# Remainders of the second MLP's weight tiles: an accumulating DMA onto a sign-turned tile in place of GpSimd's subtraction

## The chip, the cores and the metric

The kernel runs on one core of one Trainium2 chip. The metric is the device time of one execution in microseconds; the shown time is the median of three runs. One further execution was taken by the hardware profiler, and every row below is from it.

## The reference, cut to what matters

One inference step of a two-layer decoder over 512 prompt tokens and 8 x 4 sample tokens (544 columns in all), D = 1024. Layer 0 mixes by an mLSTM, layer 1 by a gated short convolution; each is followed by a squared-ReLU MLP. The change touches only the MLP of layer 1 (and the way its weights are prepared):

```
hn = modulate(x, norm_g[i, 1], mod[:, 3], mod[:, 4])
f = jnp.square(jax.nn.relu(hn @ mlp_w_up[i])) @ mlp_w_down[i]     # 1024 -> 4096 -> 1024
x = x + mod[:, 5][:, None, :] * f
```

All of it is float32.

## The kernel before

Activations lie transposed, features on the partitions and the 544 tokens along the row. Every large product is made of weight tiles of 1024 x 128 values: 192 of them, numbered `t` through the whole kernel, 8 to a unit. A float32 product is built from three products in the reduced format fp32r: the weight is split into a rounded part `wh` and a remainder `wl = raw - wh`, the activation likewise into `Xh, Xl` (or `Hh, Hl`), and TensorE adds `wh*Xh + wh*Xl + wl*Xh` into PSUM. One tile is 8 k-steps x 3 products x 2 halves of the tokens, 48 matmuls.

A weight tile passes four hands:

1. SP fetches it, 512 KB, from HBM into `raw[t % 2]` (`fetch`, L359). `raw` has two buffers (`RAWS`), so SP waits first until the remainder of tile t-2 is done (L358).
2. ScalarE rounds it: `wh[t % 4] <- raw[t % 2]` (`hi`, L465), once the tile is there and once TensorE has finished tile t-4, which held the slot (`SLOTS` = 4).
3. GpSimd subtracts: `wl[t % 4] <- raw - wh` (`lo`, L851), once step 2 is done, and signals `s_lo`.
4. TensorE waits for `s_hi` and `s_lo` of the tile (`split_wait`) and runs its 48 matmuls.

The engines' queues are in order. ScalarE's queue interleaves `hi(t+3)` (`LEAD` = 3) and the evacuation of tile t: in an up unit (relu into one of two `stage` buffers, L472 or L485) that is an activation; in a down unit ScalarE evacuates nothing, and VectorE adds the product to the residual (L1009, L1014, L1016). In an up unit VectorE squares the staged result and splits it (`drain_square`: L991, L992, L998). PSUM holds two tiles (`slot(g)`), so tile g starts only when g-2 has been evacuated.

The MLP of layer 1 is the last part of the kernel: tiles 128 to 191 (`T_MLP1` to `T_END`), eight units, up and down by turns. A unit's first two tiles run in step (`tile_pair`, matmuls at L1589), since their activations come one k at a time from VectorE; the other six run one after another (`tile`, L1563). The first up unit is special (`first_unit`): its first three tiles run on the raw x, scaled afterwards (`scale_first`), while VectorE and ScalarE still make the normalized operand (`norm_apply`, L1153, L1167; `norm_hi`, L621). GpSimd has besides one small power per norm (`norm_power`, L861).

The order of ScalarE's work in all units but the first, and the split's wait, in the kernel's words:

```
for m in range(KT):
    hi(t0 + m + LEAD, j, per_t)
    ...
    if evac is not None:
        evac(t0 + m, g0 + m, j, per_t, per_g)
```

Of the kernel before, what the change touches and what calls it, by code (L numbers as in the profile page):

```python
# [15 lines left out]
ALU = mybir.AluOpType  # L16
ACT = mybir.ActivationFunctionType
# [19 lines left out]
SLOTS, RAWS, ADAS, LEAD = 4, 2, 2, 3  # L37
# [13 lines left out]
T_CG, T_XT, T_BG, T_COUT, T_MLP1, T_MLP1_LAST, T_END = 96, 104, 112, 120, 128, 176, 192  # L51
G_QK, G_V, G_O, G_WOUT, G_MLP0, G_MLP0L, G_MLP0_LAST = 0, 8, 16, 24, 32, 48, 80
G_CG, G_XT, G_BG, G_COUT, G_MLP1, G_MLP1_LAST = 96, 104, 112, 120, 128, 176

ADA_AFTER = {1: 0, 3: 1, 5: 2, 6: 3}
ADA_AFTER_O = {2: 0, 4: 1, 5: 2, 6: 3}
ADA_AFTER_W = {1: 0, 3: 1, 4: 2, 5: 3}
# [44 lines left out]
def build_program(nc, ins, outs):  # L102
    ctx = ExitStack()
    with ctx:
# [3 lines left out]
        def sb(name, shape, dt=F32, at=None):  # L108
            n = 4
            for s in shape[1:]:  # L110
                n *= s
            n = (n + 31) // 32 * 32
            if at is None:
                at = mark["at"]
                mark["at"] += n
            return nc.alloc_sbuf_tensor_at(name, shape, dt, offset=at)
# [6 lines left out]
        def sem(name):  # L123
            return ctx.enter_context(nc.semaphore(name))
# [36 lines left out]
        raw = sb("raw", [P, RAWS, KT, P])  # L161
# [3 lines left out]
        wl = sb("wl", [P, SLOTS, KT, P], F32R, at=at_w + SLOTS * D * 4)  # L165
# [110 lines left out]
        s_au = sem("ada_tile_used")  # L276
        s_hi = sem("hi_ready")
        s_lo = sem("lo_ready")
        s_used = sem("tile_used")
        s_ev = sem("evacuated")  # L280
        s_dr = sem("drained")
# [53 lines left out]
        def at(n, j, per):  # L335

            return n if j is None else j * per + n

        def split_wait(eng, t, j, per):

            eng.wait_ge(s_hi, at(t + 1, j, per))
            eng.wait_ge(s_lo, at(t + 1, j, per))

        def ada_fetch(queue, a):

# [8 lines left out]
        def _(sp):  # L354
            def fetch(t, w, c, j=None, per=0):

                if t >= RAWS:
                    sp.wait_ge(s_lo, at(t - RAWS + 1, j, per))  # L358
                nc.sync.dma_start(raw[:, t % RAWS], w.rearrange("(k p) n -> p k n", p=P)[:, :, bass.ds(c, P)])\  # L359
                    .then_inc(s_raw[t % RAWS], 16)  # L360

            def unit(t0, w, c0, j=None, per=0, order=range(KT)):
                for m in order:
                    fetch(t0 + m, w, c0 + P * m, j, per)
# [23 lines left out]
            for a in range(H // 2):  # L388
                fetch(T_V + 3 + a, w_in, D + P * (3 + a))
                nc.sync.dma_start(C0[:, :, a, 0:DV], state_rows(ins["state_mlstm_C"][0], a)).then_inc(s_sin, 16)  # L390
# [20 lines left out]
            for a in range(H // 2):  # L411
                fetch(T_MLP0 + a, up[0], a * P)
                if a < H // 2 - 1:
                    sp.wait_ge(s_upd, SB * (a + 1))
                else:
                    sp.wait_ge(s_cud, 1)
                nc.sync.dma_start(state_rows(outs[6][0], a), C0[:, :, a, 0:DV]).then_inc(s_out, 16)
# [35 lines left out]
        def _(act):  # L453
            chain = Count(act, s_a)

            def hi(t, j=None, per=0):

                if t >= T_END:
                    return
                act.wait_ge(s_raw[t % RAWS], at(16 * (t // RAWS + 1), j, per // RAWS * 16))  # L460
                if t >= SLOTS:
                    act.wait_ge(s_used, at(t - SLOTS + 1, j, per))
                else:
                    act.wait_ge(s_au, 8)
                nc.scalar.activation(wh[:, t % SLOTS], raw[:, t % RAWS], ACT.Copy).then_inc(s_hi, 1)  # L465

            def to_stage(func, free=None, **kw):
# [109 lines left out]

            def mixed(t0, g0, n, evac, j=None, per_t=0, per_g=0, per_n=0, after={}, ada_after=ADA_AFTER, raw_of=None):

                for m in range(KT):  # L580
                    t = t0 + m
                    if t != T_QK and m != 1:
                        hi(t + LEAD, j, per_t)
                    if m == 0:
                        hi(t + 1 + LEAD, j, per_t)
                    if evac is not None:
                        evac(t, g0 + m, j, per_t, per_g)
                    if m in after:
                        after[m]()
                    if raw_of is not None and m:  # L590
                        raw_hi(raw_of, m - 1)
                    if n >= BATCH:
                        if m in BATCH_AT:
                            batch_next(n, BATCH_AT.index(m))
                    elif m in ada_after:
                        ada_next(4 * n + ada_after[m])
# [35 lines left out]
            for dst, src in pin:  # L632
# [4 lines left out]
                                 scale=-1.0).then_inc(s_silu, 1)  # L637
# [198 lines left out]
            for j in range(2):  # L836
                scale = rms[:, 1, j:j + 1]
# [5 lines left out]
        def _(pool):  # L843
            chain = Count(pool, s_p)

            def lo(t, j=None, per=0):

                if t >= T_END:
                    return
                pool.wait_ge(s_hi, at(t + 1, j, per))  # L850
                nc.gpsimd.tensor_tensor(wl[:, t % SLOTS], raw[:, t % RAWS], wh[:, t % SLOTS].bitcast(F32),  # L851
                                        ALU.subtract).then_inc(s_lo, 1)

            def lows(t0, t1, j=None, per=0):
                for t in range(t0, t1):
                    lo(t, j, per)
# [101 lines left out]
            pool.wait_ge(s_diag, 3)  # L958

            lo(T_CG + LEAD)  # L960
            pool.wait_ge(s_used, T_CG + 2)
            nc.gpsimd.memset(u[:, :, 0:2], 0.0).then_inc(s_cre, 1)
# [582 lines left out]
        def _(pe):  # L1545
# [5 lines left out]
            def tile(t, g, xh, xl, j, per_t, per_g, between=None, before_last=None):  # L1551

                s = t % SLOTS
                split_wait(pe, t, j, per_t)
                if g >= 2:
                    pe.wait_ge(s_ev, at(g - 1, j, per_g))
                for k in range(KT):
                    first, final = k == 0, k == KT - 1
                    if final and before_last is not None:
                        before_last()  # L1560
                    for w, x, st, en in ((wh, xh, first, False), (wh, xl, False, False), (wl, xh, False, final)):
                        for hf in range(2):
                            last = mm(G[:, 2 * (g % 2) + hf, 0:HALF], w[:, s, k, :], x[:, k, hf * HALF:(hf + 1) * HALF],  # L1563
                                      start=st, stop=en)
                    if final:
                        last.then_inc(s_used, 1)
                    if between is not None:
                        between(k)
# [8 lines left out]
            def pair_steps(t, g, xh, xl, width, order, free, ready, between=None):  # L1577

                for k, o in order:
                    if k == 0:  # L1580
                        split_wait(pe, t + o, None, 0)
                        free(o)
                    if o == 0:
                        ready(k)
                    s, q = (t + o) % SLOTS, 2 * ((g + o) % 2)
                    first, final = k == 0, k == KT - 1
                    for w, x, st, en in ((wh, xh, first, False), (wh, xl, False, False), (wl, xh, False, final)):
                        for hf in range(2):
                            last = mm(G[:, q + hf, 0:width], w[:, s, k, :], x[:, k, hf * width:(hf + 1) * width],  # L1589
                                      start=st, stop=en)  # L1590
                    if final:
                        last.then_inc(s_used, 1)
                    if between is not None:
                        between(k, o)
# [77 lines left out]

            def mixed(t0, g0, n, xh, xl, ready, j=None, per_t=0, per_g=0, per_n=0, post=None, between=None, ada_after=ADA_AFTER):
                for m in range(KT):
                    t = t0 + m
                    if m == 0 and ready is not None:
                        tile_pair(t, g0, xh, xl, j, per_t, per_g, ready)
                    if m > 1 or ready is None:
                        tile(t, g0 + m, xh, xl, j, per_t, per_g, None if between is None else between(m))
                        if post is not None:  # L1680
                            post(m)
                    if n < BATCH and m in ada_after:
                        ada_pair(4 * n + ada_after[m])
                if n >= BATCH:
                    ada_batch(n)
# [358 lines left out]
```

## Time and profile before

| | |
|---|---|
| time, median of 3 runs | 1353.19 us (1352.53 to 1353.42) |
| span of the profiled execution | 1352.8 us |
| TensorE (PE) busy | 1313.0 us, 97% |
| VectorE (DVE) busy | 720.8 us, 53% |
| ScalarE (ACT) busy | 361.7 us, 27% |
| GpSimd (POOL) busy | 528.5 us, 39% |
| DMA, mean | 125 GB/s |
| weight tiles in the second MLP | 64 of 192 |

PE is TensorE's matmul part and PEld its weight load. The busy share is an average over stages; a matmul's end is modelled in the profile. The span and the median differ by 0.4 us, so a sum made on the span can be read as one on the median.

### The profile page before, as it was taken

How to read it: one execution, taken by the hardware profiler on the slowest of the kernel's cores; microseconds unless marked ns; L12 is line 12 of the kernel's file. 1: busy time of each engine (PE TensorE's matmuls, PEld its weight loads, DVE VectorE, ACT ScalarE, POOL GpSimd, SP SyncE). 2: the span in 40 equal slices, each digit the busy share in tenths (PEclk: the TensorE clock that was granted, in tenths of full speed). 3: DMA queues.
4: the chain of work that ended last, by engine and by line, in shares of the span. 5: the costliest groups of instructions: out<-in, count | busy, mean ns of one | idle time of the engine just before them, and what ended most of it. 6: DMA issues, size and time to landing. Idle time of an engine off the chain costs nothing.

```text
span 1352.8 us, 26364 instructions
## 1 busy us (share of the span) xinstructions
PE 1313.0 (97%) x11593; PEld 1287.1 (95%) x11593; DVE 720.8 (53%) x1120; ACT 361.7 (27%) x560; POOL 528.5 (39%) x248
## 2 busy tenths in 40 slices
PE   5899999999999999999999999999999999999996
PEld 4799999999999999999999999999999999999996
DVE  2723445577951631541559619769861641741774
ACT  3532452121411211211222422122421221221211
POOL 2434433443343434334334344443443443433540
PEclk9899999999999999999999999999999999999998
DMA  9666214753465655555533133322223233232321
GB/s 333 193 196 155 76 53 118 237 166 117 150 194 156 185 158 157 166 166 154 170 112 94 56 101 96 88 87 78 77 80 94 80 92 94 79 93 79 94 63 66
DMA packets 239804, 169.34 MB, mean 125 GB/s; under 512 B 5691, under 2 KB 211775, under 8 KB 239562
## 3 DMA queue, kind: packets, MB, share of 16 engines
q1 hardware_dynamic: 215946, 121.33, 30.5%
q10 hardware_dynamic: 23584, 46.27, 10.5%
q8 instruction: 91, 1.49, 0.5%
q14 instruction: 23, 0.19, 0.0%
q0 software_dynamic: 160, 0.07, 0.0%
HBM read 160.70 MB, written 6.94 MB: 124 GB/s over the span
## 4 chain that ended last, share of the span: by engine, by line
PE 83%; DVE 10%; issue 3%; ACT 1%; DMA 1%; POOL 0%; SPq 0%; POOLq 0%; DVEq 0%; ACTq 0%
PE G L1563 55%; PE G L1589 20%; PE B L1659 3%; DVE hb L1153 1%; DVE acc L1030 1%; PE B L1549 1%; DVE small_s L1503 1%; DVE yc L1502 1%; DMA xin<-in_x_sample 1%; DVE Xl L1167 1%; PE B L1828 1%; DVE Hl L998 1%; DVE Hh L991 1%; PE B L1843 1%; PE B L1855 1%
## 5 line engine op out<-in xcount | busy, mean ns | idle before, releaser
L851 POOL TENSOR_TENSOR wl<-raw,wh 128x1024 fp32r<-128x1024 f32 x192 | 487.8, 2544 | 666.0 <-ACT wh L465 663.0
L465 ACT ACTIVATE wh<-raw 128x1024 fp32r<-128x1024 f32 x192 | 202.8, 1056 | 486.6 <-PE G L1563 231.9
L1563 PE MATMUL G<-Xh,wh 128*128 128x272 f32 x960 | 204.7, 295 | 1.2 <-POOL wl L851 1.2
L1563 PE MATMUL G<-Xl,wh 128*128 128x272 f32 x960 | 198.8, 288 | 0.0
L1563 PE MATMUL G<-Xh,wl 128*128 128x272 f32 x960 | 197.7, 287 | 0.0
L1563 PE MATMUL G<-Hh,wh 128*128 128x272 f32 x864 | 179.2, 289 | 0.0
L1563 PE MATMUL G<-Hl,wh 128*128 128x272 f32 x864 | 178.8, 288 | 0.0
L1563 PE MATMUL G<-Hh,wl 128*128 128x272 f32 x864 | 176.9, 286 | 0.0
L1563 PEld LDWEIGHTS G<-Xh,wh 128*128 128x128 f32 x960 | 149.8, 189 | 7.0 <-issue 4.8
L1009 DVE TENSOR_TENSOR small_s<-G,modT 128x32 f32<-128x32 f32 x80 | 15.2, 190 | 262.3 <-PE G L1563 190.3
L1563 PEld LDWEIGHTS G<-Xl,wh 128*128 128x128 f32 x960 | 151.4, 189 | 0.0
L1563 PEld LDWEIGHTS G<-Xh,wl 128*128 128x128 f32 x960 | 150.8, 189 | 0.0
L998 DVE TENSOR_TENSOR Hl<-sqb,Hh 128x544 fp32r<-128x544 f32 x72 | 143.9, 1999 | 2.5
L1563 PEld LDWEIGHTS G<-Hl,wh 128*128 128x128 f32 x864 | 136.0, 189 | 0.0
L1563 PEld LDWEIGHTS G<-Hh,wl 128*128 128x128 f32 x864 | 135.4, 188 | 0.0
L1563 PEld LDWEIGHTS G<-Hh,wh 128*128 128x128 f32 x864 | 134.7, 188 | 0.0
L991 DVE TENSOR_TENSOR Hh<-stage 128x544 fp32r<-128x544 f32 x58 | 57.2, 986 | 128.5 <-ACT stage L472 124.7
L472 ACT ACTIVATE stage<-G 128x544 f32<-128x544 f32 x64 | 40.0, 624 | 257.1 <-PE G L1563 189.6
L1563 PE MATMUL G<-Yh,wh 128*128 128x272 f32 x432 | 90.6, 291 | 0.0
L1563 PE MATMUL G<-Yl,wh 128*128 128x272 f32 x432 | 89.3, 288 | 0.0
L1563 PE MATMUL G<-Yh,wl 128*128 128x272 f32 x432 | 88.7, 286 | 0.0
L1563 PEld LDWEIGHTS G<-Yh,wh 128*128 128x128 f32 x432 | 67.3, 188 | 1.8 <-issue 1.8
(329 smaller groups left out, 2019.1 us busy)
## 6 DMA issues: line engine op xcount, KB each, us to landing
raw<-in_mlp_w_up SPq DMA_DIRECT2D x64, 512.0 KB, 4.1
raw<-in_mlp_w_down SPq DMA_DIRECT2D x64, 512.0 KB, 3.6
batch<-in_ada_w ACTq DMA_DIRECT2D x56, 512.0 KB, 5.1
raw<-in_mlstm_w_in SPq DMA_DIRECT2D x24, 512.0 KB, 4.2
raw<-in_conv_w_in SPq DMA_DIRECT2D x24, 512.0 KB, 3.7
aring<-in_ada_w ACTq DMA_DIRECT2D x22, 512.0 KB, 4.9
early<-in_ada_w SPq DMA_DIRECT2D x16, 512.0 KB, 12.3
raw<-in_mlstm_w_out SPq DMA_DIRECT2D x8, 512.0 KB, 4.9
```

The lines of the kernel that those rows point to most:

```text
L465: nc.scalar.activation(wh[:, t % SLOTS], raw[:, t % RAWS], ACT.Copy).then_inc(s_hi, 1)
L472: nc.scalar.activation(halves(stage[g % 2][:, :]), slot(g), func, **kw).then_inc(s_ev, 1)
L851: nc.gpsimd.tensor_tensor(wl[:, t % SLOTS], raw[:, t % RAWS], wh[:, t % SLOTS].bitcast(F32), ALU.subtract).then_inc(s_lo, 1)
L991: V.tensor_tensor(halves(hi_out[:, m, :]), ps, o, ALU.mult)
L998: V.tensor_tensor(lo_out[:, m, :], sqb[:, :], hi_out[:, m, :].bitcast(F32), ALU.subtract)\
L1009: mid(V.tensor_tensor(small_s[:, :].rearrange("p (h b t) -> p h b t", h=2, t=ST), ps[:, :, PH:HALF].rearrange("p h (b t) -> p h b t", t=ST ...
L1030: ins_ = V.tensor_tensor(acc[:, :], acc[:, :], sqb[:, :], ALU.add)
L1153: V.scalar_tensor_tensor(prompt(hb[k % 2][:, :]), prompt(xT[:, k, :]), gain[:, k, 0:1], prompt(xr[:, :]), ALU.mult, ALU.mult).then_inc(s_h ...
L1167: V.scalar_tensor_tensor(prompt(xl[:, k, :]), prompt(hb[k % 2][:, :]), modT[:, sh, k, 0:1], prompt(xh[:, k, :].bitcast(F32)), ALU.add, ALU ...
L1563: last = mm(G[:, 2 * (g % 2) + hf, 0:HALF], w[:, s, k, :], x[:, k, hf * HALF:(hf + 1) * HALF], start=st, stop=en)
L1589: last = mm(G[:, q + hf, 0:width], w[:, s, k, :], x[:, k, hf * width:(hf + 1) * width], start=st, stop=en)
L1659: last = mm(ada_out[GW * g:GW * (g + 1), P * quad:P * (quad + 1)], cpad[:, kk, :], columns, start=(kk == 0), stop=(kk == KT - 1), tile_pos ...
```

## The change

For tiles 128 to 191 the remainder is made in another way. ScalarE first writes the rounded tile with its sign turned into `wl` (a second activation over the same tile, ahead of the one that writes `wh`). Then GpSimd, instead of computing, issues an accumulating DMA that adds `raw` onto `wl`. Each of the four `wl` slots has a semaphore of its own; TensorE (`split_wait`) and SP (`fetch`) wait for this one in place of `s_lo`. The other 128 tiles stay as they were.

```
+T_ADDED = T_MLP1
...
+        s_lod = [sem(f"lo_added{i}") for i in range(SLOTS)]
...
             eng.wait_ge(s_hi, at(t + 1, j, per))
-            eng.wait_ge(s_lo, at(t + 1, j, per))
+            lo_wait(eng, t, j, per)
+
+        def lo_wait(eng, t, j=None, per=0):
+
+            if t >= T_ADDED:
+                eng.wait_ge(s_lod[t % SLOTS], 16 * ((t - T_ADDED) // SLOTS + 1))
+            else:
+                eng.wait_ge(s_lo, at(t + 1, j, per))
...
                 if t >= RAWS:
-                    sp.wait_ge(s_lo, at(t - RAWS + 1, j, per))
+                    lo_wait(sp, t - RAWS, j, per)
...
+                if t >= T_ADDED:
+                    nc.scalar.activation(wl[:, t % SLOTS], raw[:, t % RAWS], ACT.Copy, scale=-1.0)
                 nc.scalar.activation(wh[:, t % SLOTS], raw[:, t % RAWS], ACT.Copy).then_inc(s_hi, 1)
...
                 pool.wait_ge(s_hi, at(t + 1, j, per))
+                if t >= T_ADDED:
+                    nc.gpsimd.dma_start(wl[:, t % SLOTS], raw[:, t % RAWS], accum_op=ALU.add).then_inc(s_lod[t % SLOTS], 16)
+                    return
                 nc.gpsimd.tensor_tensor(wl[:, t % SLOTS], raw[:, t % RAWS], wh[:, t % SLOTS].bitcast(F32),
                                         ALU.subtract).then_inc(s_lo, 1)
```

## Rows read from the trace of the kernel before

**Rows 1.** Busy time by engine (us) in stretches of the second MLP.

```profile
core 0: us, PE busy (x) PEld busy (x) DVE busy (x) ACT busy (x) POOL busy (x), PEclk, DMA share, GB/s
995.00:1000.00 5.00, 3.18 (x17) 3.21 (x18) 4.72 (x6) 1.57 (x2) 2.30 (x1) 0.78 0.00 0
1000.00:1005.00 5.00, 5.00 (x37) 5.00 (x37) 2.36 (x3) 0.00 (x0) 0.42 (x1) 0.88 0.35 105
1005.00:1010.00 5.00, 5.00 (x42) 5.00 (x42) 1.14 (x4) 1.06 (x1) 1.16 (x1) 1.00 0.02 3
1046.40:1094.30 47.90, 47.49 (x380) 47.30 (x379) 29.62 (x23) 11.63 (x15) 21.24 (x8) 1.00 0.28 81
1094.30:1142.30 48.00, 47.95 (x383) 47.76 (x383) 11.75 (x24) 8.99 (x9) 19.32 (x8) 1.00 0.31 89
```

**Rows 2.** Timeline of ScalarE in an up unit: start, us, instruction, idle before.

```profile
1058.58 0.62 ACT L472 ACTIVATE stage<-G 128x544 f32<-128x544 f32 x1 [0.68 <-PE G L1589]
...
1088.58 0.62 ACT L472 ACTIVATE stage<-G 128x544 f32<-128x544 f32 x1 [4.43 <-PE G L1563]
1089.10 1.05 ACT L465 ACTIVATE wh<-raw 128x1024 fp32r<-128x1024 f32 x1
```

**Rows 3.** Timeline of GpSimd in the same unit.

```profile
1090.23 2.62 POOL L851 TENSOR_TENSOR wl<-raw,wh 128x1024 fp32r<-128x1024 f32 x1 [3.38 <-ACT wh L465]
```

**Rows 4.** Waits of SP's queue, 985 to 1345 us: total, times, longest.

```profile
SPq L359 <- POOL wl L851: 302.5, 53, 10.7
```

**Rows 5.** Fetches of L359, 1000 to 1290 us: issue to landing.

```profile
DMA to landing us min/median/max: 3.4/4.0/5.5
```

**Rows 6.** Other DMAs of the kernel: KB each, median us from issue to landing.

```profile
raw<-in_mlp_w_down SPq DMA_DIRECT2D x64, 512.0 KB, 3.6
...
xspill<-xT ACTq DMA_DIRECT2D x1, 2176.0 KB, 8.3
...
bgate<-in_mlstm_b_gates POOLq DMA_DIRECT2D x2, 0.0 KB, 5.9
crows<-in_state_conv ACTq DMA_DIRECT2D x1, 64.0 KB, 2.5
```

**Rows 7.** Timeline of GpSimd at the kernel's start: its own DMA issues.

```profile
3.40 1.16 POOL L879 DMA_DIRECT2D graw<-in_mlstm_w_in  x1 [0.30 <-POOL graw L876]
...
5.44 0.57 POOL L882 DMA_DIRECT2D bgate<-in_mlstm_b_gates  x1
```

**Rows 8.** The page: DMA engines' busy tenths in 40 slices.

```profile
DMA  9666214753465655555533133322223233232321
```

**Rows 9.** Waits of TensorE, 930 to 1353 us.

```profile
PE G L1589 <- ACT stage L485: 2.5, 1, 2.5
PE G L1589 <- ACT wh L465: 1.2, 3, 0.4
```

**Rows 10.** Timeline of VectorE in the first up unit.

```profile
972.81 2.93 DVE L992 TENSOR_TENSOR sqb<-stage 128x544 f32<-128x544 f32 x1
975.78 2.80 DVE L998 TENSOR_TENSOR Hl<-sqb,Hh 128x544 fp32r<-128x544 f32 x1
978.69 0.72 DVE L991 TENSOR_TENSOR Hh<-stage 128x544 fp32r<-128x544 f32 x1
...
995.23 0.72 DVE L998 TENSOR_TENSOR Hl<-sqb,Hh 128x544 fp32r<-128x544 f32 x1
```

**Rows 11.** Timeline of ScalarE in the first up unit.

```profile
971.38 1.05 ACT L465 ACTIVATE wh<-raw 128x1024 fp32r<-128x1024 f32 x1
...
978.92 1.06 ACT L465 ACTIVATE wh<-raw 128x1024 fp32r<-128x1024 f32 x1 [2.67 <-DMA raw<-in_mlp_w_down]
983.13 0.63 ACT L485 ACTIVATE stage<-G 128x544 f32<-128x544 f32 x1 [3.15 <-DVE Hl L998]
...
996.05 0.62 ACT L485 ACTIVATE stage<-G 128x544 f32<-128x544 f32 x1 [6.83 <-DVE Hl L998]
```

**Rows 12.** Timeline of TensorE at the first down unit's start.

```profile
996.82 0.49 PE L1589 MATMUL G<-Hh,wh 128*128 128x272 f32 x2 [2.45 <-ACT stage L485]
```

## The prediction

> **What bounds the kernel now.** I read the page first, then the busy time by stretches, then the waits of TensorE, of SP's queue and of the three other engines, and last the timelines of one unit in the middle of the second MLP and of its first up unit. TensorE is the bound: a unit of eight tiles takes 47.9 to 48.0 us and TensorE is busy for 47.5 to 47.95 of them, at full granted clock [rows 1]. So a tile costs 48.0 / 8 = 6.0 us, and all else has to keep up with one tile per 6.0 us. Over the whole stretch TensorE waits little: 2.5 us once at the end of the first up unit and three times 0.4 us where an up unit follows a down unit [rows 9]. Nothing that GpSimd does is awaited by TensorE directly, so taking 64 subtractions off GpSimd frees nothing on the path by itself.
>
> The work around the change is a ring. In the steady part ScalarE evacuates a tile at 1088.58, rounds the next one at 1089.10 (1.05 us) [rows 2], GpSimd subtracts from 1090.23 for 2.62 us, to 1092.85 [rows 3], and that frees the raw buffer for SP: its queue stands 302.5 us in 53 waits for just this [rows 4]. The fetch then lands after a median of 4.0 us [rows 5] (3.6 for the down weights of the whole kernel [rows 6]); I take 3.9. Rounding, a hop of 0.08, 2.62 and 3.9 make 7.7 us. There are two raw buffers, so a buffer may take two tiles' time, 12.0 us, for one round. It has 4.3 us to spare.
>
> **The change part by part.** *Removed:* GpSimd's 2.6 us per tile from the ring. *Added:* a second activation over the tile. It has the shape of the present one, so 1.05 us, ahead of the round-off, 64 times. ScalarE is busy for 11.6 us of 47.9 in an up unit [rows 1]; 8.4 more fit. The ring gets 1.05 us of it. *Added:* the adding DMA, from GpSimd's wait to its landing; call it X. The round is then 2 x 1.05 + 0.1 + X + 3.9 = 6.1 + X, and it fits into 12.0 us as long as X is under 5.9. Beyond that each microsecond of X costs half a microsecond per tile, 32 per kernel. All hangs on X, and the trace before has no adding DMA and none from SBUF to SBUF.
>
> Bounds for X. *Fixed part:* the shortest landings are 2.5 us for 64 KB issued from ScalarE's queue [rows 6]; GpSimd's issue of a DMA takes 0.57 us for one with few pieces and 1.16 us for one with many [rows 7]. A whole tile has 128 rows, few, so 2.5 + 0.6 = 3.1. The 5.9 us of GpSimd's own tiny DMAs [rows 6] were measured while the engines were 90% busy [rows 8]; I keep 5.9 as the upper end of the fixed part. *Moving:* a fetch of 512 KB takes the 16 engines 0.29 of 6.0 us = 1.75 us (share of the two units in rows 1). The large store, 2176 KB in 8.3 us, gives (2176 - 64) / (8.3 - 2.5) = 364 KB/us, or 1.4 us for 512 KB [rows 6]. An add reads the source and the old contents and writes once. If the reads overlap it takes 1.4 us, as two passes 3.5 us, as three 5.25 us. So X lies between 2.5 + 1.4 = 3.9 and 5.9 + 5.25 = 11.2 us. I take 3.1 + 3.5 = 6.6, two passes at the fetch's own rate, because that is the one rate measured in this stage and each byte that is added has to be read twice.
>
> The Trainium skill's page "DMA: Bandwidth & Descriptors" (section Anatomy of one DMA) fits 2.0 us plus bytes at 436 GB/s, 3.2 us for a tile, and "Collectives: The Full Stack" (section on large sizes) holds that an add in the DMA engines runs at half a copy's rate for its two source reads, which makes some 4.4 us by these pages (an estimate). No row here shows an add. By it the sum would be no loss; that outcome is a rival below.
>
> *Moved together:* the add of one buffer and the fetch into the other now share the 16 engines. With X = 6.6 the add of one tile and the fetch half a round later coincide for some of their 3.5 and 1.75 us of engine time. Fully overlapped, each is held up by what it shares, up to 1.8 us a round; kept apart, nothing. I take 0.5 us. The round becomes 6.1 + 6.6 + 0.5 = 13.2 us, 1.2 over, and there are some 30 of them in series on a buffer (32, less the first, fetched ahead, and the last, which nothing follows): 30 x 1.2 = 36 us.
>
> Slack in hand pays back a part. The second tile of a pair is needed 0.75 us after the pair's start, and its slot was freed 12 us before that start; its remainder is ready 0.5 + 2.1 + 0.1 + 6.6 + 0.5 = 9.8 us after that, 3 us early. So 3 us of lateness go by once before TensorE stands. 36 - 3 = 33 us.
>
> *The other waits that the change adds.* Behind ScalarE's longer wait for raw tiles stands the evacuation of a tile, and behind that VectorE's drain and TensorE's PSUM slot; an evacuation may be late by about 5.4 us (6.0 less 0.62) before the tile after next stands, so in the steady part the missing remainder ends first, not this. Near a pair the first two tiles end 2.25 us apart (the evacuation at 1058.58 had but 0.68 us of idle before it [rows 2]), so the two adds are issued close together and partly share the engines; that is within the 0.5 above. GpSimd's queue holds nothing else in the stage but two tiny powers; it only waits and issues.
>
> *What VectorE gains.* VectorE's operations on 128x544 take 0.72 us with GpSimd idle and 2.8 to 2.93 us while it subtracts [rows 10]. In the first up unit five such long ones stand in the chain of drains that delays the evacuation at 996.05 [rows 11], and TensorE stands 2.45 us for it [rows 12]. After that the granted clock is 0.78 and 0.88 for 10 us (a part of that time at the lower of its two levels), and 17 and 37 matmuls run where 26 (in the 3.2 us left of the stretch) and 41 to 42 would [rows 1]: 9 and 4.5 lost, at 0.125 us each 1.7 us. Together 4.1 us. With no subtraction the drains end some 10 us earlier and this wait goes, provided the weights are there. In that unit the ring is already late before: the round-off at 978.92 waited 2.67 us for its fetch [rows 11]. Following it: round-off at 971.38, now done at 973.5, add landed at 973.6 + X, fetch 3.9, round-off done at 979.6 + X, add landed at 979.7 + 2X, next fetch, and the round-off ahead of the evacuation of the last tile ends at 985.7 + 2X. That evacuation, 0.6 us, must be done by 996.8 - 2.45 = 994.4, so the 4.1 us are only won if X is at most 4.0; at X = 5 about half, at 5.9 nothing. At X = 6.6 what TensorE waits for are remainders, and I count no gain.
>
> The sum on the profiled span: 1352.8 + 33 = 1386; on the median the same to half a microsecond.
>
> **Rivals.**
> *A, the forecast:* the ring is over its 12.0 us by 0.5 to 3 us. 30 x 0.5 - 3 = 12 and 30 x 3 - 3 = 87, so 1365 to 1440, likeliest 1386. Chance 0.42.
> *B, hidden:* X with sharing is between 4.3 and 6.0 us. The lateness is taken by the slack, and a gain of 0 to 2.5 us in the first up unit stands against a few tenths of wait at pairs. 1350.5 to 1355. For it speaks the 3.1 us fixed part with 1.4 of moving, 4.5 us. Chance 0.26.
> *C, faster:* one mechanism, at the end of the first up unit: VectorE is no longer held up by GpSimd, the wait of 2.45 us and the slower clock after it go. It decides where X is 4.0 us or less: 1353.2 - 4.1 = 1349. Against it, that X must be at its lower bound. Chance 0.13. The skill's rule above (4.4 us) falls between B and C.
> *D, far over:* the fixed part for GpSimd's DMAs is really near the 5.9 us of [rows 6]: X = 5.9 + 3.5 = 9.4, with sharing a round of 16.0 us: 30 x 4.0 - 3 = 117, so about 1470, and 1520 at the upper bound. Against it, those DMAs stood in full queues. Chance 0.19.
> That the add is not made as a DMA in the background, but holds GpSimd, changes nothing: GpSimd has no other work here.
>
> **How the numbers follow.** The forecast is A's, 1386. The range takes in all of B and A and the near part of D and leaves out most of C and D's far part: 1350 to 1460, with A's own 1365 to 1440. Under 0.2%, 2.7 us, a measurement can't tell a change. Faster by more than that: 0.12, most of C. Within: 0.27, B and the rest of C. Slower: 0.61, A and D.
>
> **What would show it.** In the profile after: 64 more activations of 1.05 us at the line of the sign-turned copy; GpSimd nearly idle over the last third; VectorE's L998 at 0.72 us throughout; SP's queue waiting for the adds; the landing time of the adds, which is X (right near 6.6); ScalarE's round-off waiting for raw DMAs in nearly every tile instead of for TensorE; TensorE waiting for the adds' landing at most tiles, and a unit of 51 to 56 us. The prediction is wrong if X is under 5.9 us (units stay at 48 us), or if the adds and fetches slow each other much more than 0.5 us, or if standing for a part of each tile costs TensorE its clock, as it did after 996.

## The result and the profile after

The changed kernel takes 1370.67 us in the median of seven runs, against 1353.42 us for the kernel before, also of seven: 17 us or 1.3% slower. The ratio, which leaves out the longest run of the changed kernel (1386.9 us) as one of a slower state, is 1.010, with a 95% interval of 1.0063 to 1.0138, or 14 us. The two kernels differ in their spread too: the one before lies within 1352.5 to 1355.0 us, the changed one between 1359 and 1387 us. The direction was forecast, the size (33 us) was not.

The profiled execution took 1378.96 us with a span of 1377.2, so it is one of the longer ones: 24.4 us over the span of before. First the page: busy time by engine, TensorE's granted clock and the DMA engines' share in 40 slices, and GpSimd's own DMA queue.

```profile
PE 1319.8 (96%) x11593; PEld 1294.0 (94%) x11593; DVE 639.9 (46%) x1120; ACT 421.5 (31%) x624; POOL 420.7 (31%) x248
...
PEclk9999999999999999999999999999999999999998
DMA  9665213762663653653622332335667777778772
...
q0 software_dynamic: 9376, 33.63, 13.7%
...
raw<-in_mlp_w_up SPq DMA_DIRECT2D x64, 512.0 KB, 4.4
raw<-in_mlp_w_down SPq DMA_DIRECT2D x64, 512.0 KB, 4.0
wl<-raw POOLq DMA_DIRECT2D x64, 512.0 KB, 5.3
```

VectorE is busy for 81 us less with the same 1120 instructions: the last of its three operations per drain (L998, now L1012) takes 0.72 us each time, where it took 2.4 us in the mean from 998 to 1310 us of the kernel before. ScalarE has 60 us more. The DMA engines go from two or three tenths [rows 8] to seven in the last third. The adding DMA, the unknown of the prediction, lands 5.3 us after its issue in the median, and the fetches beside it 4.4 and 4.0 us. The add's engine time is 13.7% of 1377.2 us over 64, that is 2.95 us of all 16 engines.

Next the waits of 930 to 1377 us by engine and releaser: total, times, longest; one row of SP's queue, two of ScalarE's, then TensorE's.

```profile
SPq L368 <- DMA wl<-raw: 382.1, 61, 10.5
...
ACT wl L475 <- DMA raw<-in_mlp_w_down: 112.7, 20, 8.9
...
ACT wl L475 <- DMA raw<-in_mlp_w_up: 78.8, 20, 8.9
...
PE G L1603 <- DMA wl<-raw: 14.1, 4, 5.5
PE G L1603 <- ACT stage L483: 5.2, 2, 3.0
PE G L1603 <- ACT stage L496: 2.2, 1, 2.2
```

ScalarE, which waited for TensorE before each round-off [rows 2], now waits for fetches 40 times, and the fetches wait for adds. TensorE's waits are few and long: four for adds, 14.1 us in all, and three for evacuations, 7.4 us, all at L1603, the pairs at a unit's start. That the lateness of six tiles comes due there, since both tiles of a pair are wanted together, is how I read it; no run tests it. Counted from the first matmul of a pair to that of the next, the units from 993 to 1309 us take 54.2, 55.6, 50.8, 54.3, 52.6 and 48.7 us. Before, they took 52.2 and then 48.7 or 48.3.

The chain that ended last in the stretch from 1060 to 1145 us, in order of time, shows the ring itself. Columns: start, us, what.

```profile
1072.20 7.21 DMA wl<-raw
1079.40 0.01 issue
1079.42 4.39 DMA raw<-in_mlp_w_up
...
1086.13 6.54 DMA wl<-raw
...
1099.34 0.02 ACT wl L475
1099.37 0.07 issue
1099.44 0.02 ACTq L471
1099.45 0.85 issue
1100.31 1.05 ACT wh L476
1101.36 0.28 issue
1101.64 4.53 DMA wl<-raw
1106.17 0.02 issue
1106.19 6.34 DMA raw<-in_mlp_w_down
1112.53 0.02 issue
1112.56 1.06 ACT wl L475
```

From 1069.90 to 1138.22 no matmul is in the chain, only one raw buffer's negate, round-off, add and fetch, five rounds of 12.5 to 15.5 us where 12.0 are allowed. Such a chain picks the later buffer; the other one's rounds in the same stretch take 12.0 to 13.0 us, read from GpSimd's issues. The one shown in full takes 13.2 us, 1099.34 to 1112.56. Its add takes 4.5 us, the shortest seen, and its fetch 6.3, against 3.5 at its shortest; two rounds earlier it is the add that takes 7.2 us and the fetch 4.4. The timeline of GpSimd, with the adds of both buffers, tells why.

```profile
1072.20 0.84 POOL L863 DMA_DIRECT2D wl<-raw  x1 [3.75 <-ACT wh L476]
1079.70 0.86 POOL L863 DMA_DIRECT2D wl<-raw  x1 [6.66 <-ACT wh L476]
...
1101.64 0.84 POOL L863 DMA_DIRECT2D wl<-raw  x1 [8.32 <-ACT wh L476]
1105.13 0.85 POOL L863 DMA_DIRECT2D wl<-raw  x1 [2.64 <-ACT wh L476]
1114.85 0.84 POOL L863 DMA_DIRECT2D wl<-raw  x1 [8.87 <-ACT wh L476]
```

In the up unit the two buffers lie about half a round apart, 7.5 us, and the add of 1072.20 meets the other buffer's fetch, which SP issues at 1072.33. In the down unit they have drawn together, 3.5 us, and the second add, of 1105.13, falls first into the other add and then into the first buffer's fetch of 1106.19. They meet either way.

Last the busy time by stretches, of the changed kernel around one wait, and over six units; the row by itself is the same 300 us of a kernel that does not wait (first12_raw3, below). The columns are those of [rows 1].

```profile
1045.00:1055.00 10.00, 4.49 (x31) 4.30 (x31) 1.04 (x3) 3.90 (x4) 1.70 (x2) 0.80 0.67 142
1055.00:1060.00 5.00, 5.00 (x32) 5.00 (x31) 0.00 (x0) 1.32 (x2) 0.00 (x0) 0.72 0.92 223
...
1000.00:1300.00 300.00, 284.98 (x2214) 284.05 (x2214) 68.78 (x135) 103.67 (x115) 38.35 (x46) 0.97 0.74 162
```

```profile
1000.00:1300.00 300.00, 298.61 (x2378) 297.49 (x2378) 132.75 (x152) 65.32 (x74) 127.12 (x50) 1.00 0.30 89
```

In those 300 us TensorE runs 164 matmuls fewer than where it does not wait, 20.5 us at 0.125 us each. It is idle for only 13.6 us more. The other 7 us are the clock: after the wait of 5.5 us, which ends at 1053.61, the granted clock of the next 5 us is 0.72, so a part of them ran at the lower of the two levels (1.2 GHz instead of 2.4), and 32 matmuls ran where 42 do. Where TensorE does not stand, in the row of first12_raw3, the granted clock is 1.00.

### The profile page after: what moved, and what is told of

The parts are those of the page before. It is cut to its first block, busy times and chain, and to the rows that moved or that the text cites. A ratio compares the mean times of both kernels' runs of the same rounds, so it can differ in the third digit from the quotient of the medians.

```text
span 1377.2 us, 26428 instructions
## 1 busy us (share of the span) xinstructions
PE 1319.8 (96%) x11593; PEld 1294.0 (94%) x11593; DVE 639.9 (46%) x1120; ACT 421.5 (31%) x624; POOL 420.7 (31%) x248
## 3 DMA queue, kind: packets, MB, share of 16 engines
q0 software_dynamic: 9376, 33.63, 13.7%
## 4 chain that ended last, share of the span: by engine, by line
PE 63%; DMA 21%; DVE 7%; issue 4%; ACT 4%; SPq 0%; POOL 0%; POOLq 0%; DVEq 0%; ACTq 0%
PE G L1577 38%; PE G L1603 16%; DMA wl<-raw 9%; DMA raw<-in_mlp_w_down 6%; DMA raw<-in_mlp_w_up 4%; PE B L1673 3%; ACT wh L476 2%; PE B L1563 1%; DVE small_s L1517 1%; ACT wl L475 1%; DVE yc L1516 1%; DMA xin<-in_x_sample 1%; DVE hb L1167 1%; PE B L1842 1%; DVE acc L1044 1%
## 5 line engine op out<-in xcount | busy, mean ns | idle before, releaser
L865 POOL TENSOR_TENSOR wl<-raw,wh 128x1024 fp32r<-128x1024 f32 x128 | 325.2, 2544 | 440.7 <-ACT wh L476 438.8
L863 POOL DMA_DIRECT2D wl<-raw x64 | 54.7, 854 | 357.6 <-ACT wh L476 345.4
L1005 DVE TENSOR_TENSOR Hh<-stage 128x544 fp32r<-128x544 f32 x58 | 51.2, 883 | 203.5 <-ACT stage L483 188.0
L475 ACT ACTIVATE wl<-raw 128x1024 fp32r<-128x1024 f32 x64 | 67.7, 1057 | 225.8 <-DMA raw<-in_mlp_w_down 112.7
L1012 DVE TENSOR_TENSOR Hl<-sqb,Hh 128x544 fp32r<-128x544 f32 x72 | 94.1, 1307 | 2.5
```

Of the source, the lines that this page charges most:

```text
L475: nc.scalar.activation(wl[:, t % SLOTS], raw[:, t % RAWS], ACT.Copy, scale=-1.0)
L863: nc.gpsimd.dma_start(wl[:, t % SLOTS], raw[:, t % RAWS], accum_op=ALU.add).then_inc(s_lod[t % SLOTS], 16)
L1005: V.tensor_tensor(halves(hi_out[:, m, :]), ps, o, ALU.mult)
L1012: V.tensor_tensor(lo_out[:, m, :], sqb[:, :], hi_out[:, m, :].bitcast(F32), ALU.subtract)\
```

## The experiments

My theory at this point: the round of a raw buffer is longer than two tiles' time, by latency. The rivals: the DMA engines are short of throughput; the second activation on ScalarE is what costs; the expensive part is a DMA issued from GpSimd as such, not its adding. All times are medians, with the ratio to the kernel before on the same chip and its 95% interval.

**a_raw3: a third raw buffer for tiles 128 on.** It lies where `aring` was, dead in this part of the kernel; tile 130 finds it free, and tiles 131 on wait for the remainder of tile t-3.

```
+RAWS1 = 3
...
+        raw1 = sb("raw1", [P, RAWS1, KT, P], at=at_raw)
+
+        def raw_of_tile(t):
+            return raw1[:, (t - T_MLP1) % RAWS1] if t >= T_MLP1 else raw[:, t % RAWS]
```

> The changed kernel with three raw buffers in the second MLP (the third lies in the space of a buffer that is dead by then). Ring theory: the changed kernel lost because a raw buffer's round (negate and round off 2.0 us, add 4.5 to 7.2 us, fetch 3.5 to 6.6 us, seen as 12.5 to 15.5 us) does not fit into two tiles, 12.0 us; three buffers allow 18 us, so TensorE does not wait for weights any more and the time falls to 1349 to 1353 us, at best with the 4.1 us of the first up unit won. Engine theory (the 16 DMA engines cannot carry the adds beside the fetches): a third buffer only lets more of both queue up; the time stays at 1360 to 1380 us. ScalarE theory (the second activation delays evacuations): no change either, 1360 to 1380 us.

1347.81 us, 0.9958 (0.9946 to 0.9971): not only the loss is gone, it is 5.6 us faster than before. Its waits of TensorE from 930 to 1345 us are these two rows, and the second is at the very end:

```profile
PE G L1614 <- DVE xT L1039: 1.2, 3, 0.4
PE G L2036 <- DVE acc L1055: 0.6, 1, 0.6
```

From 1000 to 1300 us the adds (first line) and the fetches (second line) land no earlier than in the changed kernel, where their medians were 5.4 and 4.6 us, and the DMA engines carry more per microsecond (172 GB/s against 162):

```profile
DMA to landing us min/median/max: 4.5/5.7/8.2
...
DMA to landing us min/median/max: 3.5/4.7/8.1
```

So neither throughput nor the second activation is what failed: the same adds, somewhat slower ones even, are harmless where a round may take 18 us.

**b_raw3: the third raw buffer in the kernel before.** The same edit without the adds.

```
-                    sp.wait_ge(s_lo, at(t - RAWS + 1, j, per))
...
+                    sp.wait_ge(s_lo, at(t - back + 1, j, per))
```

> Control: the kernel before with the same third raw buffer. Its ring has 4.3 us to spare, so all theories expect no change, 1351 to 1354 us. If it gained, the third buffer would be worth something of its own and a_raw3 would have to be read against it.

1353.84 us, 1.0004 (0.9995 to 1.0014). The buffer has no worth of its own, and the wait of 2.4 us at the end of the first up unit stays. TensorE's granted clock stays at 1.00 after it, where it fell to 0.78 after the 2.45 us of the kernel before [rows 1]: the clock's price does not follow each such wait.

**neg_only: the second activation alone, in the kernel before.**

```
+                if t >= T_MLP1:
+                    nc.scalar.activation(wl[:, t % SLOTS], raw[:, t % RAWS], ACT.Copy, scale=-1.0)
                 nc.scalar.activation(wh[:, t % SLOTS], raw[:, t % RAWS], ACT.Copy).then_inc(s_hi, 1)
```

> The kernel before with only the added activation: the sign-turned tile is written and then overwritten by GpSimd's subtraction. Ring theory: the round is 7.7 + 1.0 = 8.7 us, under 12.0, so no change in the steady part, 1352 to 1356 us with a microsecond or two in the first up unit, where the ring was late before. ScalarE theory: most of the loss of the change, 1360 us and more.

1354.91 us, 1.0008 (0.9999 to 1.0017): 1.5 us, if anything. The ScalarE theory falls.

**plain_copy: the add as a plain copy.** The remainder is replaced by the whole tile.

```
-                    nc.gpsimd.dma_start(wl[:, t % SLOTS], raw[:, t % RAWS], accum_op=ALU.add)...
+                    nc.gpsimd.dma_start(wl[:, t % SLOTS], raw[:, t % RAWS])...
```

> The changed kernel with a plain DMA copy of raw onto the tile in place of the adding one (the remainder is then the whole tile, so this computes something else). It keeps issue, size and both waits and takes away only the second read and the addition. If accumulating is the expensive part (ring and engine theory alike): the landing falls from 5.3 us to some 3.5 to 4 us, the engines' share from 0.7 to about 0.55, and the time to 1349 to 1356 us. If a DMA issued by GpSimd is slow for its issue and its fixed part, the landing stays above 4.5 us and the time above 1358 us.

1349.9 us, 0.9972 (0.9962 to 0.9982). The page's rows on GpSimd's queue and its landing:

```profile
q0 software_dynamic: 9376, 33.63, 7.6%
...
wl<-raw POOLq DMA_DIRECT2D x64, 512.0 KB, 3.4
```

Adding costs 1.9 us of landing in the median (5.3 against 3.4), 1.6 us at the shortest (4.5 against 2.9), and nearly doubles the engine time: 7.6% of 1347.5 us over 64 is 1.60 us, against 2.95. The Trainium skill's page "Collectives: The Full Stack" (section "The bandwidth ceiling: the fold count and why AG ≠ RS ≠ AR") gives an add two source reads and half a copy's rate, a factor of two; the ratio here is 1.84. GpSimd's issue as such was not the trouble. At the end of the first up unit a wait of 1.2 us for the evacuation is left.

**half_add: an add over half the tile.** The remainder of four k-slices is left at the negative rounded tile.

```
+                    nc.gpsimd.dma_start(wl[:, t % SLOTS, 0:KT // 2], raw[:, t % RAWS, 0:KT // 2], accum_op=ALU.add)...
```

> The changed kernel with an adding DMA over four of the eight k-slices, 256 KB in place of 512 KB (the remainder of the other four stays the negative rounded tile, so this computes something else). It splits the landing into a fixed and a moving part. By the prediction's terms (3.1 fixed, 3.5 moving) it would land in 3.1 + 1.75 = 4.9 us; by the 4.5 us that an add took alone in the changed kernel and 2.4 us of it fixed, in 3.4 to 3.8 us. Ring theory: the round falls under 12 us in either case, and the time to 1348 to 1354 us.

1349.32 us, 0.9963 (0.9948 to 0.9978). The adds of 1000 to 1300 us:

```profile
DMA to landing us min/median/max: 3.2/3.7/5.8
```

The shortest landing is 3.2 us for 256 KB and 4.5 for 512 KB. That makes 1.3 us per half, so by these two shortest landings 2.6 us of moving and 1.9 us fixed for an undisturbed add. As with the plain copy, a wait of 1.2 us for the evacuation at the end of the first up unit is left.

**early_add: GpSimd issues the add before the second round-off.** Only the wait moves; SP waits for both.

```
+                    nc.scalar.activation(wl[...], raw[...], ACT.Copy, scale=-1.0).then_inc(s_neg, 1)
...
+                    pool.wait_ge(s_neg, t - T_ADDED + 1)
...
+                    if t - RAWS >= T_ADDED:
+                        sp.wait_ge(s_hi, t - RAWS + 1)
```

> The changed kernel, but GpSimd issues the add as soon as the sign-turned tile is there, while ScalarE still rounds off the second time (the add does not read that tile). SP waits for both before it fetches over the raw tile. Ring theory: the round of a raw buffer gets 1.0 us shorter, which is more than half of what it is over 12.0 us in the median, so most of the loss goes: 1350 to 1362 us, against 1360 to 1380 for the changed kernel. Engine theory (throughput, not latency): no change, 1360 to 1380 us, since as many bytes are moved.

1351.82 us, 0.9984 (0.9976 to 0.9993). One microsecond less of latency, with not a byte less to move, takes away 19 of 1371 us (16 by the ratios) and the spread with it (1348.5 to 1353.7). That is the low end of what I had expected: the ring lies near its limit. From 1000 to 1300 us TensorE loses nothing:

```profile
1000.00:1300.00 300.00, 298.61 (x2378) 297.49 (x2378) 78.97 (x154) 113.20 (x124) 42.14 (x50) 1.00 0.80 173
```

The evacuation at the end of the first up unit is still late, so the gain of that unit is not won:

```profile
PE G L1607 <- ACT stage L499: 2.9, 1, 2.9
```

**one_buffer: adds for even tiles only.** Odd tiles, in the other raw buffer, are subtracted.

```
+        def added(t):
+            return t >= T_ADDED and t % 2 == 0
```

> The changed kernel with the adding DMA only for even tiles (one of the two raw buffers); odd tiles are subtracted by GpSimd as before. Ring theory with contention as the missing part: an add never meets another add and meets a fetch more rarely, so it lands in 4.5 to 5.3 us and its ring (2.0 + 0.3 + 5 + 4 = 11.3 us) fits, the other ring needs 7.7 us: no wait for weights, 1351 to 1356 us. If the add were over 6 us by itself, the even ring would stay over 12 us and TensorE would still wait, half as much or more: 1360 us and up.

1353.75 us, 0.9999 (0.999 to 1.0008). The page's row for the adds:

```profile
wl<-raw POOLq DMA_DIRECT2D x32, 512.0 KB, 4.6
```

With no other add to meet, the landing is 4.6 us in the median (4.5 from 1000 to 1300 us), so the add alone is a 4.5 us operation and its ring fits. What is gone here is the other buffer's adds; its fetches are still there. So what lengthened an add in the changed kernel was the other buffer's traffic, most likely its adds. How much the other buffer's fetches lengthen an add no run separates.

**first12_raw3: three raw buffers, adds for tiles 128 to 139 only.**

```
+        def added(t):
+            return T_ADDED <= t < T_ADDED + 12
```

> Three raw buffers, and the adding DMA only for tiles 128 to 139, that is for the first up unit; from tile 140 on GpSimd subtracts. If the gain of a_raw3 (5.6 us) comes from VectorE running free of GpSimd in the first up unit and in the norm before it, as I hold, all of it is here too: 1347 to 1349 us. If the later units gave a part, the time lies between that and 1353 us.

Tiles 128 to 135 are the first up unit's own; the next four are prepared while it runs or just after it.

1348.26 us, 0.9961 (0.9946 to 0.9977): all of the gain of a_raw3 is in the first up unit and the norm before it; the other 52 adds give nothing. The units of a_raw3's trace say the same: the first two take 51.2 and 48.3 us against 52.7 and 52.2 before, the rest as long as before.

**first12: the same with two raw buffers.**

> The same with the two raw buffers of the kernels before and after. By the prediction's step, the evacuation at the end of the first up unit is in time only if the add lands in 4.0 us; measured were 4.5 to 5.7. So part of the gain: 1349 to 1354 us. A ring that is over its time for 12 tiles only costs at most 2 or 3 us.

1355.7 us, 1.0015 (1.0006 to 1.0024), slower than before and above the range I gave. TensorE's waits are these:

```profile
PE G L1607 <- ACT stage L500: 2.9, 1, 2.9
PE G L1607 <- DMA wl<-raw: 2.5, 1, 2.5
```

The wait for the evacuation stays, and one of 2.5 us for an add is new. With two buffers the first up unit gets worse by the change, not better.

**a_raw4: four raw buffers.** `RAWS1 = 4`.

> Four raw buffers in place of three: 24 us for a round. Ring theory: three were enough, so the same as a_raw3, 1347 to 1349 us. If a_raw3 was still held up in places by its ring, up to 1 us less.

1347.52 us, 0.995 (0.9933 to 0.9967), the same as with three.

**early_raw3: three raw buffers and the early add.**

> Three raw buffers and the add issued before the second round-off: the two remedies together. Ring theory: each alone removes the lateness, so they do not add up: 1347 to 1349 us, the same as three buffers alone.

1347.31 us, 0.9947 (0.9932 to 0.9962), the same again. The remedies don't add up: each takes away the same lateness. With a_raw3 and a_raw4 these are versions that beat both kernels, the one before by 5.6 to 7.4 us, each against runs of it on the same chip.

**side_adds: the adds' traffic beside the old ring.** In the kernel before, GpSimd issues after each subtraction an adding DMA between two dead buffers. No other engine waits for it; GpSimd itself waits for the last one before it issues the next.

```
+                if t >= T_MLP1:
+                    if t > T_MLP1:
+                        pool.wait_ge(s_side, 16 * (t - T_MLP1))
+                    nc.gpsimd.dma_start(aring[:, 1], aring[:, 0], accum_op=ALU.add).then_inc(s_side, 16)
```

> The kernel before, in which GpSimd also issues, after each subtraction of the second MLP, an adding DMA of 512 KB between two buffers that are dead by then; nothing waits for it but the next one's issue. The DMA engines carry the same bytes as in the changed kernel, but the add is outside the round of a raw buffer. Ring theory: the round is 7.7 us plus up to 3 us of fetches made longer by the adds, under 12.0 us, so no loss: 1352 to 1357 us, with fetches landing in 4.5 to 5 us instead of 4.0. Engine theory (too much traffic): 1360 to 1380 us as in the changed kernel.

1356.93 us, 1.0015 (1.0003 to 1.0026). Its busy time and its add's landing:

```profile
1000.00:1300.00 300.00, 298.60 (x2362) 297.49 (x2362) 110.83 (x149) 63.91 (x73) 162.24 (x98) 0.99 0.75 173
```

```profile
aring<-aring POOLq DMA_DIRECT2D x64, 512.0 KB, 5.3
```

The fetches from 1000 to 1300 us:

```profile
DMA to landing us min/median/max: 3.5/4.1/5.6
```

The DMA engines are as full as in the changed kernel, the adds land as late, and TensorE loses 2 us in all, at the top of what I expected. The engine theory falls by this run and by a_raw3. One expectation failed: the fetches land after 4.1 us, not 4.5 to 5, and earlier than the 4.6 of the changed kernel. So the same bytes beside a fetch do not always cost it the same.

## Why the prediction was right or wrong

*The step that failed: the size of a round.* The sum took 13.2 us for the round of a raw buffer, 1.2 us over what it may take, 30 times. Measured from the negate of a tile to the landing of the fetch that refills its buffer, the 47 rounds that start from 1000 to 1300 us of the profiled execution take 12.6 us in the mean, so 0.6 us over, half of the 1.2. They spread from 11.1 to 17.2 us, and 30 of the 47 are over 12.0; so not every round was late, as the 30 x 1.2 had it. The terms: 6.6 + 0.5 + 3.9 = 11.0 us were taken for add, sharing and fetch, and the mean landings are 5.4 and 4.8, 10.2 us; activations and hops were taken at 2.2 and take 2.3.

*The ring, its limit and who waits for whom: right in the main.* The raw buffer's round bounds the stage, 12.0 us is what it may take, and more buffers lift it (a_raw3), a microsecond less does (early_add), and so does taking the adds out of it (side_adds). Most signs named for the trace are there: ScalarE waits for fetches, VectorE's long operations are gone, GpSimd only issues, and five of the six units from 993 to 1309 us take 50.8 to 55.6 us, where 51 to 56 were named. Two are not. The adds do not land near 6.6 us. And TensorE waits for an add four times, not at most tiles; it stands at pairs alone, three times for evacuations, which the prediction had behind the remainders (7.4 us against 14.1).

*X alone: too long.* I took 3.1 fixed and 3.5 moving, 6.6 us. The runs show 1.9 and 2.6, 4.5 us (half_add, one_buffer). The fixed part was priced by landings with HBM at one end and by GpSimd's issue added in full; the moving part by two passes at the fetch's rate for 512 B pieces, 1.75 us each, where one plain pass of this shape takes 1.60 us of engine time and the add 2.95. By the prediction's own terms and this X alone, a round is 2.0 + 0.3 + 4.5 + 3.5 = 10.3 us at its shortest and would have fitted: rival B would have been the answer. The estimate worked out from the Trainium skill's two pages, 4.4 us, was nearer than my choice; it lies inside B's bounds, not between B and C as I wrote.

*The sharing: too short.* I took 0.5 us between bounds of 0 and 1.8. The mean round is 2.3 us over the undisturbed 10.3, and the five rounds of the chain from 1069.90 to 1138.22 take 13.7 us each, 3.3 over. My upper bound was wrong. It priced one meeting a round, where a buffer's add can meet the other's add or fetch and its fetch the other's add as well. The round from 1083.83 to 1099.34 is 5.2 us over, and the longest, from 1014.72, 6.9. So X was 2.1 us too long, the fetch 0.4 us (3.9 against 3.5) and the sharing 1.8 us too short in the mean. That the forecast round comes as near as it does, 13.2 against 12.6, is luck: errors of opposite sign.

*What the lateness costs TensorE.* 30 rounds of 0.6 us make 18 us, less the slack. After 930 us TensorE waits 22.5 us in all, against 5.3 in the kernel before: 17.2 us more. The clock adds 7 us; it was named as a risk and not priced. Together they make nearly all of the 24.4 us of this profile. On GpSimd's count, from tile 128's turn to tile 191's, there are 31.5 rounds, 390.5 us before (923.6 to 1314.1) and 417.0 us after (924.0 to 1341.1). In the median the loss is 17 us: that the rounds meet more or less often from run to run, and that this makes the spread, is argued and not shown, since only one execution was profiled, and one of the longer ones; it agrees with early_add, where most of the spread is gone too.

*The first up unit: right in mechanism.* The evacuation behind a late round-off was to cost the 4.1 us gain unless X was 4.0 or less. In the changed kernel TensorE waits 2.2 us for just this evacuation (L496). The wait is 2.9 us with the early add, 1.2 us with the plain copy and the half add, whose landings are 3.4 and 3.6 us, and it is gone with three buffers. So the limit on X lies lower than 4.0. And by my own chain of times each microsecond of X makes the evacuation 2 us later, so half of the wait is back at 4.7 and all of it at 5.3, not at 5 and 5.9. Rival C's mechanism is real, with 5.6 us instead of 4.1: the short waits in the norm before it, 1.0 us in all, go too. Its condition was not met by the change as made. The 1.7 us of clock in the 4.1 are less certain, since the clock did not fall after the same wait in b_raw3.

## What to carry to other kernels

When work moves from an engine to a DMA, time the loop of buffers that it stands in, not the engine that is relieved: here 2.6 us of subtraction became 1.05 + 0.3 + 4.5 to 7 us of latency in a loop with 4.3 us to spare. An uncontended latency that fits is not enough if two such loops run on one set of DMA engines; their meeting was worth 2.3 us a round in the mean and 6.9 at the most seen, as much as the error in the operation's own price (2.1). One more buffer, where space lies dead, turned the loss of 17 us into a gain of 6; an issue that waits for what it needs and no more turned it into a gain of 2. The gain that was to be had sat in one unit of eight, where VectorE was on the path.

## What the runs showed of the hardware

- An adding DMA of 512 KB within SBUF, 128 rows of 4 KB, lands after 4.5 us at the shortest, a plain one after 2.9 (medians in use 5.3 and 3.4); they take 2.95 and 1.60 us of the 16 engines' time. GpSimd's issue takes 0.85 us for the adding one, for the half-sized one too, and 0.53 us for the plain one.
- In this profile the two loops did not come to a spacing in which they miss each other: 6.3 to 7.5 us apart in one unit and 1.9 to 3.5 us in the next, with rounds of 12.0 to 15.5 us. Later, from 1211 us on for example, the adds come in pairs 2.4 us apart: the first lands after 4.5 us, the second after 5.5, and the fetches behind them after 5.2 and 4.6. The worst case seen is an add of 1023.27 and a fetch of 1023.49: they land after 8.5 and 8.4 us. Even with the other's whole engine time on top of its shortest landing, the add would take 4.5 + 1.75 = 6.3 us and the fetch 3.5 + 2.95 = 6.5 us. What makes the rest is open.
- VectorE's operations on two inputs in SBUF that took 2.7 to 2.95 us beside GpSimd's subtraction take 0.72 us beside an add, in the traces read here.
